# One hybrid decoder layer: the second feed-forward matmul as seven block products in 15 of 16 chunks, between half slabs of the next chunk's first matmul

## What is computed

```
mod = c_act @ w_ada[l] + b_ada[l]
sh1, sc1, gt1, sh2, sc2, gt2 = jnp.split(mod, N_MOD, axis=-1)
...
y = jnp.concatenate([rms_norm(y_lru, ...), rms_norm(y_att, ...)], axis=-1) @ w_out[l]
x = x + gt1[:, None, :] * rms_norm(y, g_post_mix[l])
h = modulate(rms_norm(x, g_pre_mlp[l]), sh2, sc2)
y = jnp.square(jax.nn.relu(h @ w_ff1[l])) @ w_ff2[l]
x = x + gt2[:, None, :] * rms_norm(y, g_post_mlp[l])
```

## Time and profile before

| | us |
|---|---|
| median of 3 runs | 2311.75 (2310.22 to 2312.07) |
| span of the profiled execution | 2307.4 |
| PE busy in it | 2207.3 |
| DVE busy | 1163.0 |
| ACT busy | 666.6 |
| POOL busy | 149.0 |

### The profile page before, as it was taken

How to read it: one execution, slowest core, us unless ns; L and a number is a source line. 1 busy time by engine, 2 the same in 40 slices (tenths; PEclk the granted TensorE clock), 3 DMA queues, 4 the chain that set the end, 5 groups by cost and what they waited for, 6 DMA issues and landing times.

```text
span 2307.4 us, 24341 instructions
## 1 busy us (share of the span) xinstructions
PE 2207.3 (96%) x9441; PEld 1762.1 (76%) x9441; DVE 1163.0 (50%) x1410; ACT 666.6 (29%) x897; POOL 149.0 (6%) x134
## 2 busy tenths in 40 slices
PE   4779999999889989999999999999999999999998
PEld 3557778888667778778888888888888888888886
DVE  7998695456884657843332332422332342333335
ACT  4224622222553253222222312311221221221232
POOL 3451040000120000000000000000000000000000
PEclk7889999999999999999999999999999999999999
DMA  9874456637425645842333223233223223323342
GB/s 332 287 231 152 141 188 195 189 116 261 132 87 183 219 144 179 274 133 83 106 95 91 92 92 98 82 105 95 91 92 98 92 91 94 97 91 92 99 165 91
DMA packets 178308, 321.49 MB, mean 139 GB/s; under 512 B 12184, under 2 KB 47112, under 8 KB 176192
## 3 DMA queue, kind: packets, MB, share of 16 engines
q1 hardware_dynamic: 172576, 303.12, 41.3%
q0 software_dynamic: 3408, 16.92, 2.2%
q10 hardware_dynamic: 2256, 0.53, 0.1%
HBM read 312.13 MB, written 8.40 MB: 139 GB/s over the span
## 4 chain that ended last, share of the span: by engine, by line
PE 84%; DVE 11%; ACT 3%; issue 2%; DMA 1%; DVEq 0%; ACTq 0%
PE bank L356 14%; PE bank L357 14%; PE bank L358 14%; PE bank L368 13%; PE bank L367 13%; PE bank L366 13%; DVE acc L1068 6%; DVE LP L1203 1%; DVE stat L1198 1%; DVE w_lo L1039 0%; DVE yg L1313 0%; PE bank L530 0%; DVE LP L1195 0%; ACT w_hi L712 0%; ACT junk L941 0%
## 5 line engine op out<-in xcount | busy, mean ns | idle before, releaser
L1331 DVE TENSOR_TENSOR w_lo<-raw,w_hi 128x1024 fp32r<-128x1024 f32 x253 | 308.3, 1223 | 704.2 <-ACT w_hi L986 703.8
L356 PE MATMUL bank<-h_hi,w_lo 128*128 128x512 f32 x1536 | 620.0, 404 | 17.1 <-POOL h_lo L1457 10.8
L357 PE MATMUL bank<-h_lo,w_hi 128*128 128x512 f32 x1536 | 614.7, 400 | 0.0
L358 PE MATMUL bank<-h_hi,w_hi 128*128 128x512 f32 x1536 | 614.2, 400 | 0.0
L986 ACT ACTIVATE w_hi<-raw 128x1024 fp32r<-128x1024 f32 x253 | 267.0, 1059 | 980.4 <-PE bank L368 487.0
L368 PE MATMUL bank<-w_hi,u_hi 128*128 128x512 f32 x1024 | 408.4, 399 | 0.0
L367 PE MATMUL bank<-w_lo,u_hi 128*128 128x512 f32 x1024 | 403.5, 394 | 0.0
L366 PE MATMUL bank<-w_hi,u_lo 128*128 128x512 f32 x1024 | 402.9, 393 | 0.0
L356 PEld LDWEIGHTS bank<-h_hi,w_lo 128*128 128x128 f32 x1536 | 293.6, 191 | 93.7 <-issue 17.7
L357 PEld LDWEIGHTS bank<-h_lo,w_hi 128*128 128x128 f32 x1536 | 293.4, 191 | 71.6 <-issue 1.4
L358 PEld LDWEIGHTS bank<-h_hi,w_hi 128*128 128x128 f32 x1536 | 293.0, 191 | 71.9
(11 more groups left out here) (215 smaller groups left out, 1638.8 us busy)
## 6 DMA issues: line engine op xcount, KB each, us to landing
raw<-in_w_ff_dram SPq DMA_DIRECT2D x256, 512.0 KB, 3.7
raw<-in_w_ada_dram SPq DMA_DIRECT2D x128, 512.0 KB, 4.6
raw<-in_w_in_dram SPq DMA_DIRECT2D x82, 512.0 KB, 3.9
gst<-in_w_ada_dram SPq DMA_DIRECT2D x64, 512.0 KB, 6.0
raw<-in_w_out_dram SPq DMA_DIRECT2D x32, 512.0 KB, 4.5
x_tok<-in_x_dram SPq DMA_DIRECT2D x4, 1024.0 KB, 8.3
xr<-in_x_dram POOLq DMA_DIRECT2D x4, 1024.0 KB, 7.0
x_scratch<-yg POOLq DMA_DIRECT2D x4, 1024.0 KB, 4.7
```

The source lines that it names most:

```text
L356: pe.matmul(b[:, :], lo[:, cols], act_hi[:, kt, :], start=(kt == 0), stop=False)
L357: pe.matmul(b[:, :], hi[:, cols], act_lo[:, kt, :], start=False, stop=False)
L358: last = pe.matmul(b[:, :], hi[:, cols], act_hi[:, kt, :], start=False, stop=(kt == n_kt - 1))
L1331: dve.tensor_tensor(w_lo[:, s], raw[:, slot], w_hi[:, s].bitcast(F32), ALU.subtract).then_inc(lo_ready, 1)
```

## The change

- 16 chunks of 512 hidden columns instead of 8 of 1024. The last chunk keeps the plain second matmul, 8 units of 24 matmuls.
- In chunks 0 to 14 the second matmul is taken as 2x2 blocks: 256 + 256 hidden columns, 256 + 256 tokens, 1024 + 1024 output columns (these in two rounds r of 512 columns each). Instead of eight block products there are seven (Strassen, in Winograd's form) for each r, 14 in a chunk. A product is 12 matmuls into a pair of banks (`product`). It needs sums of weight blocks (`w2_total`, four for each r, DVE, in the buffer `acc` as `w2_x` or in `raw`), sums of token blocks (`operand_total`, four a chunk, DVE) and their high and low parts (`operand_high` on ACT, `operand_low` on DVE). DVE adds each product from the two banks into `y2` (`read_product`; one product for each r goes into two places). Some products keep on accumulating in their banks.
- PE goes through half slabs (`w1_piece`: one k-tile of the next chunk's first matmul, 12 matmuls) between products: `W_BEFORE` says how many stand ahead of each of the 14. `w_hi`/`w_lo` slots 2 and 3 and a new two-slot buffer `w1_raw` serve the first matmul, slots 0 and 1 and `raw` the second. `W_MADE` says after which product a first-matmul unit is split.
- Relu goes from a pair of banks at once into `u_raw` (`rectify`), the square stays there (`square_u`).
- Chunk 0's first matmul stands ahead of the loop (192 matmuls). The ada units: two after each of 16 output projection units, instead of one; 16 are left for chunk 0's first matmul, two for each unit of `w_ff1`.
- Gates 4 to 7 are no longer 128 rows in `G2`; a single row is multiplied, stored to DRAM and read back broadcast near the end (`store_gate2`, `g2_scr`). The gate matmuls stand elsewhere: 4 in the projection, 5 in the last mixing round, 6 and 7 in chunk 0's first matmul. POOL clears `y2` with a memset.

```diff
-    CHUNKS = 8
-    FT = D_FF // CHUNKS // P
-    assert (S, D, DH, KT, NT, CT, FT, CW, HEADS, LB) == (512, 2048, 128, 16, 4, 8, 8, 4, 8, 64)
+    CHUNKS = 16
+    FF = D_FF // CHUNKS
+    FT = FF // P
...
-        return (U_ATT + 2 <= n < U_OUT + 2) + (U_OUT + 3 <= n < U_OUT + 19) + 2 * (U_MLP + 8 <= n < U_MLP + 24)
+        return (U_ATT + 2 <= n < U_OUT + 2) + 2 * (U_OUT + 3 <= n < U_OUT + 19)
...
+    HALVES = KT
+    PRODUCTS = 14
+    W_BEFORE = [1, 1, 1, 1, 1, 1, 1, 1, 1, 1, 2, 2, 2, 0]
+    W_MADE = {1: 2, 3: 3, 5: 4, 7: 5, 9: 6, 10: 7, 11: 8, 13: 9}
+    assert sum(W_BEFORE) == HALVES
+    A11, S_1, S_2, S_4, S_3, A12, A22 = range(7)
+    SUM_OF = {1: 1, 2: 2, 4: 3, 6: 4}
+    READS_BEFORE = [0, 1, 2, 3, 4, 6, 7]
...
+            sp.wait_ge(y_sum, 4)
+            for j in range(8):
+                if j >= 2:
+                    sp.wait_ge(w1_lo, j - 1)
+                load_w1((0, 0), j)
+                for pos in (POS_MLP + 2 * j, POS_MLP + 2 * j + 1):
+                    load(pos)
+            for j in range(2):
+                sp.wait_ge(w1_lo, 7 + j)
+                load_w1((1, 0), j)
+            for which in range(4):
+                sp.wait_ge(ada_used, N_ADA - (len(stream) - 1 - which) % RING)
+                load_w2((0, 0), 0, which)
+            for j in (2, 3):
+                sp.wait_ge(w1_lo, 7 + j)
+                load_w1((1, 0), j)
+            sp.wait_ge(w2_sum, 1)
+            load_w2((0, 0), 1, 0)
...
+            def product(ck, n, first=False):
+                r, i = divmod(n, 7)
+                pe.wait_ge(w2_lo, of(ck, PRODUCTS, n + 1))
+                if r == 0:
+                    pe.wait_ge(op_lo_ready, of(ck, 7, i + 1))
+                if n:
+                    before = 8 * ((n - 1) // 7) + READS_BEFORE[(n - 1) % 7]
+                    if before or not first:
+                        pe.wait_ge(product_read, of(ck, 16, before))
+                elif not first:
+                    pe.wait_ge(product_read, of(ck, 16, -1))
+                bank = pairs[2 + (i + r) % 2]
+                fresh = i in (0, 1, 5, 6)
+                for k in range(2):
+                    hi, lo = w_tile(n % 2, k)
+                    for tt in range(2):
+                        tok = slice(tt * P, (tt + 1) * P)
+                        pe.matmul(bank[:, tt, :], op_lo[:, i, k, tok], hi, start=(fresh and k == 0), stop=False, skip_group_check=True)
+                        pe.matmul(bank[:, tt, :], op_hi[:, i, k, tok], lo, start=False, stop=False, skip_group_check=True)
+                        last = pe.matmul(bank[:, tt, :], op_hi[:, i, k, tok], hi, start=False, stop=(k == 1), skip_group_check=True)
+                last.then_inc(product_done, 1)
+            def iteration(ck, first=False):
+                q = 0
+                for n in range(PRODUCTS):
+                    for _ in range(W_BEFORE[n]):
+                        if q == 0:
+                            pe.wait_ge(relu_done, of((ck, 1), 2, 0))
+                        w1_piece((ck, 1), q)
+                        q += 1
+                    product((ck, 0), n, first)
+            pe.wait_ge(x1t_copied, 4 * (NT - 1))
+            for q in range(HALVES):
+                pe.wait_ge(h2_lo_ready, q + 1)
+                w1_piece((0, 0), q)
+                if q == 11:
+                    pe.wait_ge(x1t_copied, 4 * NT)
+                    row_job(22, pairs[2][:, 0, :])
+            row_job(23, pairs[3][:, 0, :])
+            pe.wait_ge(gate_ready, 8)
+            iteration(0, first=True)
+            with pe.Fori(1, CHUNKS - 2) as ck:
+                iteration(ck)
+            iteration(CHUNKS - 2)
...
+            def next_operands(ck, first=False):
+                rectify(ck, 0, first)
+                rectify(ck, 1, first)
+                square_u(ck, 0)
+                w2_high(ck, 0, first)
+                operand_high(ck, A11, first)
+                square_u(ck, 1)
+            def iteration(ck, first=False, last=False):
+                for n in range(PRODUCTS):
+                    if n < 5:
+                        operand_high((ck, 0), n + 2, first)
+                    if n in W_MADE and not (last and W_MADE[n] >= 8):
+                        w1_high((ck, 1), W_MADE[n])
+                    if n < PRODUCTS - 2:
+                        w2_high((ck, 0), n + 2)
+                    elif n == PRODUCTS - 2 and not last:
+                        next_operands((ck, 1))
+                    elif n == PRODUCTS - 1 and not last:
+                        operand_high((ck, 1), S_1)
+                        w2_high((ck, 1), 1)
...
+            def iteration(ck, first=False, last=False):
+                for n in range(PRODUCTS):
+                    if n < 6:
+                        operand_low((ck, 0), n + 1)
+                    if n < 3:
+                        operand_total((ck, 0), n + 2)
+                    if n == PRODUCTS - 1 and not last:
+                        operand_low((ck, 1), A11)
+                        operand_total((ck, 1), S_1)
+                    read_product((ck, 0), n, first)
+                    if n < PRODUCTS - 2:
+                        w2_low((ck, 0), n + 2)
+                    elif not last:
+                        w2_low((ck, 1), n + 2 - PRODUCTS)
+                    if n + 3 < PRODUCTS:
+                        if (n + 3) % 7 in SUM_OF:
+                            w2_total((ck, 0), n + 3)
+                    elif not last and n + 3 - PRODUCTS in SUM_OF:
+                        w2_total((ck, 1), n + 3 - PRODUCTS)
+                    if n in W_MADE and not (last and W_MADE[n] >= 8):
+                        w1_low((ck, 1), W_MADE[n])
...
+                    w1_low((0, 0), (kt - 3) // 2 + 2)
+                    for a in (0, 1):
+                        ada_unit(ADA_MLP + kt - 3 + a)
+                if kt == 13:
+                    take_gate(6, pairs[2][:, 0, :])
+            for a in (N_ADA - 2, N_ADA - 1):
+                ada_unit(a)
+            take_gate(7, pairs[3][:, 0, :])
+            w2_low((0, 0), 0)
+            w2_total((0, 0), 1, first=True)
+            operand_low((0, 0), A11)
+            operand_total((0, 0), S_1)
+            w2_low((0, 0), 1)
+            w2_total((0, 0), 2)
+            w1_low((0, 0), 9)
+            iteration(0, first=True)
+            with dve.Fori(1, CHUNKS - 2) as ck:
+                iteration(ck)
+            iteration(CHUNKS - 2, last=True)
...
+            pool.wait_ge(x1t_done, 4 * NT)
+            pool.memset(y2[:, :, :], 0.0).then_inc(y2_zero, 1)
+            store_gate2(6)
+            load_gain(7)
+            store_gate2(7)
+            pool.wait_ge(g2_stored, 64)
+            pool.wait_ge(w1_used, 8 * CHUNKS)
+            pool.dma_start(G2[:, :], g2_scr[0:1, :].to_broadcast([P, D])).then_inc(g2_in, 16)
```

More of the change, by code:

```diff
@@ L224, in col, with of @@
             return vcol[:, base + i:base + i + n]
+        w_ff23 = w_ff22.rearrange("(c f) n -> c f n", f=FF)
+        def of(ck, per, n):
+            loop, later = ck
+            return loop * per + (later * per + n)
         block = ctx.enter_context(nc.Block())
@@ L332, in _ @@
+            iteration(0)
+            with sp.Fori(1, CHUNKS - 2) as ck:
+                iteration(ck)
+            iteration(CHUNKS - 2, w1_next=False)
+            for e, which in enumerate(LAST_ORDER):
+                sp.wait_ge(w2_lo, LAST * PRODUCTS + e + 1)
+                load_w2((LAST, 0), 1, which)
             for t in range(NT):
@@ new lines, in _, with last_unit @@
+            row_job(23, pairs[3][:, 0, :])
[4 more added lines that the diff above has]
+            iteration(CHUNKS - 2)
+            def last_unit(e, tiles=range(NT)):
+                half = e % 2
+                for k in range(2):
+                    hi, lo = w_tile((2, 3, 0, 1)[e % 4], k)
+                    for t in tiles:
+                        bank = pairs[e // 2 % 2 * 2 + t // 2][:, t % 2, :]
+                        i, tok = ((A11, A12), (S_1, A22))[t // 2][half], slice(t % 2 * P, (t % 2 + 1) * P)
+                        pe.matmul(bank, op_lo[:, i, k, tok], hi, start=(half == 0 and k == 0), stop=False)
+                        pe.matmul(bank, op_hi[:, i, k, tok], lo, start=False, stop=False)
+                        done = pe.matmul(bank, op_hi[:, i, k, tok], hi, start=False, stop=(half == 1 and k == 1))
+                return done
@@ L1019, in _ @@
+            last_high(4)
+            last_high(5)
+            for t in range(NT):
+                final_square(0, t)
+            last_high(6)
+            last_high(7)
+            for g in (1, 2):
+                for t in range(NT):
+                    final_square(g, t)
             for t in range(NT):
```

535 lines of the change are left out of this document (321 added, 214 removed).

## The result

The changed kernel took 2318.16 us, the median of 7 runs (2317.22 to 2322.1), beside 2311.11 us (2308.76 to 2312.07) for the kernel before. The ratio is 1.0034, with a 95% interval of 1.0024 to 1.0044: **slower by 0.3%**, where I had forecast 2300 us and faster. The profiled execution of the changed kernel has a span of 2319.1 us; 1.8 us lie outside it.

The account below looks back on a forecast made before the run. PE's matmuls were taken to bound the kernel (busy 96%). Terms -84.0 +15 +41.5 +3.0 +0.9 -2.1 +4.4 +9.4 = -11.9 gave a span of 2295.5, forecast 2300 us with 4.4 outside it; range 2270 to 2325.

Parts of the forecast that it names:

- Matmuls removed: Second matmul: 360 fewer matmuls at 0.2333 us each, as PE never waits; -84.0 us.
- Rival (4): Products don't give a matmul's time each, for banks or waits: 0.02 us a matmul, +50, 2350 us; chance 0.03.
- The projection rounds: Output projection with doubled ada units: DVE full, rounds slip about a microsecond, PE's weights 16.8 us ahead; 0, up to 8.
- The memset: GpSimd's clearing of the accumulator, 7.6 us beside DVE's first modulations: 0, or 7.6 if it held DVE up throughout.
- The start round: First chunk's first matmul: closed round of load, cast, low part and two ada units, 11.7 us, six times; +41.5 us.
- Start of the passes: Ahead of the first pass: second matmul's first blocks load only after ada slots are free; +3.0 us.
- The loop: Turn of each pass: DVE's operand 3 late by 0.6; 1.0 us a pass taken, 15 passes, +15 us.
- Rival (3): Turn of each pass: the DVE-ACT-DVE chain loses 3 us or more a pass; 2330 us at 3, slower; chance 0.17.
- Last chunk: Between product 13 and the last chunk's first unit: PE waits 3.9 us for DVE, plus 0.5 for clock; +4.4 us.
- tail: Kernel's end: a tile's last group has 12 matmuls instead of 24, DVE needs 5.26 us a tile; +9.4 us.
- Gates and mix tail: Gate 5 in the last mixing round +0.9 us; four gate matmuls gone from the first chunk's PE stream -2.1 us.

## Why the prediction was wrong

By its own steps, with the spans of the two profiles: I said 2295.5, it was 2319.1, 23.6 more. The profiled execution was 2.7 us above the median of its kernel. In it 2.9 us were there already at the first gate matmul of the projection, 705.37 instead of 702.45, ahead of everything that the steps below count; the kernels with the same code up to there had it at 702.12 to 705.76, so at least part of that is chance. (The 4.4 us that I took outside the span were too many: 1.8 lie outside the changed kernel's, and the profiled run of before was a short one.)

- **Matmuls removed, -84.0: right.** A pass without its wait is 84.23 us, and leaving 11 more matmuls out gives 2.58 a pass. Rival (4) is refuted.
- **The projection rounds, 0: this step failed.** The first h_hi part comes at 881.11 instead of 856.49 us, 24.6 later. I had 0.9 of it and 2.9 lie ahead of the stage, so 20.8 are this step's. I reasoned "PE's weights are three units, 16.8 us, ahead" and that DVE would slip a microsecond a round. Two waits in the code say otherwise. The lead was the wrong one: PE also waits for a gate product at the head of a round, and that was only 4.7 us ahead in the kernel before. And the slip is not set by how full DVE is, but by a wait: a sum's first step needs the gate matmul of two sums before, which has a fixed place in PE's stream. The kernel before has the wait too, once from 640 to 860 us and for 3.6 us; in the changed one it is 20.7 us in three. Before, ada steps came once a unit; at twice the pace DVE came to the next sum of a buffer while PE still had units to do ahead of the matmul that reads the old one. DVE is the engine that waits, ada slots and SP's queue stand behind it, and one wait of 13.06 us is far more than a lead of 4.7. With the third buffer the memset starts 20.0 us earlier (880.56 to 860.54), of which 2.1 lie ahead of the stage (705.37 to 703.25) and 17.9 in it. My bound of 8 was for the x loads only and was too small for that reason too.
- **The memset, 0: failed, 5.2.** I had written "if it held DVE up throughout it would cost 7.6" and took 0 because DVE's modulations are ahead of PE. The first one isn't: PE waits for it. The bound was right and the choice between its ends was not.
- **The start round, 41.5 (41.4 by its own figures): the mechanism right, the exact sum lucky.** 11.7 us a round by sum, 11.71 measured on average, six of them. But two of its parts were off by 1.1 us each, in opposite directions: from a cast to the next load's issue I had 6.9 and it was 5.78, since only the second of the two ada loads waits for the second ada unit; from the issue to the cast I had 4.8 and it was 5.9. Other runs of the same code had 11.1 to 11.6 on average. The stage took 3.6 us more than the 86.4 from 859.6 to 946.0. Of these, 2.5 are that the cast of unit 2 waits for 24 matmuls that now partly ran at the 1.2 GHz level, 0.43 us apart, behind the memset's pause (897.01 is 8.42 behind the first half slab; I had 5.95 to 864.69), and 1.1 that gate 7's matmul and product took 2.8 us instead of 1.7. That the order in SP's queue makes the round, not the transfers, is shown by the loads moved ahead.
- **Start of the passes, +3.0: right.** Product 0 starts 984.36, 5.79 behind 978.57; 2.8 + 3.0 were forecast. PE's own wait is only 0.81 of it, since the half slab ahead ran at a granted clock of 0.58; DVE's operand part sets the time either way.
- **The loop, +15: right place, a third of the size.** At product 3, as counted, but 0.36 us a pass instead of 1.0, some 5 us in all. My reserve for register instructions was not needed. Rival (3), the chain at 3 us a pass, is refuted, yet its mechanism is real: an added step of 0.6 us cost 0.60.
- **Last chunk 4.4: right but for 1.0; tail 9.4: right.** The wait was 3.75 where 3.9 were forecast. The matmuls at the 1.2 GHz level behind it cost 1.6 us (14 from start to start take 4.88 instead of 3.27), and I had 0.5. From group 2's last matmul, which I put 0.26 ahead of the adds at 2290.06 as in the prediction, to the end are 29.3 us, and 29.3 were forecast.
- **Gates and mix tail: not told apart.** They lie inside the 24.6 us above.

Together: 2295.5 + 2.9 (ahead of the stage) + 20.8 (projection) + 5.2 (memset) + 3.6 (start stage) + 1.0 (last chunk) - 10 (loop) = 2319.0, within 0.1 of the span; so close a sum is itself partly luck. The two terms that I had put at nought, 26 us, turned the sign; a loop better than feared gave over a third of that back. That the time lay in my range was luck in this sense, and no rival of mine was what happened. Each looked at the loop or the start stage, and none at the stage in which the change only moved work.
